# The rotary half exchange of the prompt's queries on ScalarE instead of TensorE, and a later wait for parked rows, in a one-layer hybrid decoder step

## The reference, cut to what matters

```python
def rope(x, pos):
    half = ROPE_DIM // 2                      # 32
    ...
    x1, x2 = x[..., :half], x[..., half:]
    return jnp.concatenate([x1 * cos - x2 * sin, x1 * sin + x2 * cos], axis=-1)

q = jnp.einsum('bsc,chd->bshd', rmsnorm(qa, g_q_a), w_q_b)       # 16 heads of 128 + 64
q_nope, q_pe = q[..., :NOPE_DIM], rope(q[..., NOPE_DIM:], q_pos)
...
# PEER: the 2048 numbers of a token are projected to 8 heads x 2 x 128 query numbers,
# each scored against 128 sub keys; the 16 best of each half are combined
q = jnp.einsum('td,dhpk->thpk', hb, w_peer_query)
s = jnp.einsum('thpk,hpnk->thpn', q, peer_sub_keys)
s1, i1 = lax.top_k(s[:, :, 0], PEER_TOPK)
s2, i2 = lax.top_k(s[:, :, 1], PEER_TOPK)
```

## Time and profile before

| | us |
|---|---|
| median of 3 runs (lowest, highest) | 4596.78 (4593.75, 4599.67) |
| the profiled execution's own time | 4598.26 |
| its span on the core | 4596.5 |

### The profile page before, as it was taken

How to read it: one execution, slowest core, us unless ns; L and a number is a source line. 1 busy time by engine, 2 the same in 40 slices (tenths; PEclk the granted TensorE clock), 3 DMA queues, 4 the chain that set the end, 5 groups by cost and what they waited for, 6 DMA issues and landing times.

```text
span 4596.5 us, 37965 instructions
## 1 busy us (share of the span) xinstructions
PE 3684.4 (80%) x13918; PEld 2303.6 (50%) x13918; DVE 2780.5 (60%) x3641; ACT 392.1 (9%) x882; POOL 1493.0 (32%) x1217
## 2 busy tenths in 40 slices
PE   8999999987999999999999999999999980000000
PEld 6888846652999585555555456444444430000000
DVE  3224323431000168887676578888965569999998
ACT  1012123321000010000000010000000000000000
POOL 0000100024000013444454445434332227777763
PEclk9999999998999999999999999999999995555555
DMA  4121261137667678998999989999999999999998
GB/s 167 65 74 65 102 235 42 42 126 251 230 239 245 230 289 309 395 400 366 403 421 411 367 366 388 403 406 403 395 412 393 423 423 409 401 410 410 410 412 364
DMA packets 223666, 1413.36 MB, mean 307 GB/s; under 512 B 33312, under 2 KB 42400, under 8 KB 59488
## 3 DMA queue, kind: packets, MB, share of 16 engines
q0 software_dynamic: 137424, 904.11, 48.5%
q1 hardware_dynamic: 72768, 471.37, 26.9%
q10 hardware_dynamic: 13296, 35.52, 2.0%
HBM read 1385.11 MB, written 25.75 MB: 307 GB/s over the span
## 4 chain that ended last, share of the span: by engine, by line
PE 71%; DMA 13%; POOL 5%; issue 5%; DVE 4%; ACT 1%; SPq 0%; ACTq 0%; DVEq 0%; POOLq 0%
PE psum L975 25%; PE psum L1116 13%; PE psum L627 12%; DMA arena<-in_v,arena 12%; PE psum L1095 4%; POOL arena L582 3%; DVE psum L2062 3%; POOL arena L602 2%; PE psum L1080 2%; PE psum L1043 1%; PE psum L1023 1%; PE psum L699 1%; PE psum L709 1%; PE psum L869 1%; PE psum L868 1%
## 5 line engine op out<-in xcount | busy, mean ns | idle before, releaser
L975 PE MATMUL psum<-arena 128*128 128x160 f32 (+1 forms) x5120 | 1175.7, 393 | 1.0 <-DVE arena L1746 0.8
L975 PEld LDWEIGHTS psum<-arena 128*128 128x128 f32 x5120 | 835.7, 190 | 340.5 <-DVE arena L1746 0.9
L2062 DVE SCALAR_TENSOR_TENSOR psum<-arena,psum 128x2048 f32<-128x2048 f32 x381 | 897.1, 2355 | 165.2 <-DMA arena<-in_v,arena 155.7
L582 POOL DMA_INDIRECT arena<-in_v,arena x544 | 648.4, 1192 | 744.0 <-DVE psum L2062 327.1
L1116 PE MATMUL psum<-arena 128*128 128x512 f32 x2048 | 881.8, 593 | 0.6 <-ACT arena L1433 0.6
L582 POOL DMA_INDIRECT arena<-in_u,arena x288 | 479.2, 1664 | 1228.3 <-DVE arena L1853 516.2
L1116 PEld LDWEIGHTS psum<-arena 128*128 128x128 f32 x2048 | 390.0, 190 | 491.9 <-issue 491.9
L627 PE MATMUL psum<-arena 128*128 128x272 f32 x2432 | 562.0, 392 | 0.9 <-issue 0.9
L627 PEld LDWEIGHTS psum<-arena 128*128 128x128 f32 x2432 | 460.8, 190 | 98.8 <-issue 5.5
L1940 DVE SCALAR_TENSOR_TENSOR arena<-arena,pages 128x2048 f32<-128x2048 f32 x128 | 301.1, 2352 | 72.1 <-DMA arena<-in_v,arena 67.3
L1897 DVE CUSTOM_DVE_ANT_1 arena<-arena 128x2048 f32<-128x2048 f32 x128 | 288.5, 2289 | 55.8 <-DMA arena<-in_u,arena 54.8
(11 more groups left out here) (298 smaller groups left out, 2678.6 us busy)
## 6 DMA issues: line engine op xcount, KB each, us to landing
arena<-in_w_merge SPq DMA_DIRECT2D x160, 1024.0 KB, 5.6
arena<-in_u_cols SPq DMA_DIRECT2D x128, 1024.0 KB, 9.3
arena<-in_w_out SPq DMA_DIRECT2D x32, 1024.0 KB, 4.9
arena<-in_w_query SPq DMA_DIRECT2D x32, 1024.0 KB, 6.9
arena<-in_w_proj SPq DMA_DIRECT2D x31, 1024.0 KB, 4.9
products<-arena ACTq DMA_DIRECT2D x32, 512.0 KB, 13.6
arena<-in_pool_keys SPq DMA_DIRECT2D x64, 192.0 KB, 3.6
arena<-in_v,arena POOLq DMA_INDIRECT x544, 12.0
```

The costliest lines, as they stand in the source:

```text
L582: pool.indirect_dma_start(row, None, A[table], bass.IndirectOffsetOnAxis(ap=idx[:, r:r + 1], axis=0))\
L975: last = mm(out, w[:, (off + k) * P:(off + k + 1) * P], src[:, k0 + k, lo:hi], start=(k == 0), stop=(k == n - 1))
L2062: V.scalar_tensor_tensor(a, four(row), atmp_b[:, t, r:r + 1], a if r else four(x1_b[:, t, :]), ALU.mult, ALU.add).then_inc(s("rows_used"), 1)
```

## The change

1. The two permutation matmuls of a pair are gone. `values(0, 2)` now carries the ring signal that the first of them carried, and `values(2, 4)` follows at once.
2. ScalarE copies `pair(3)` four times, 32 partitions by 544 columns each, into `ropt` with the halves exchanged, ahead of its copy to `qraw`. VectorE waits for `q_stored` instead of `q_swapped`, and its first operation reads and writes `ropt` in SBUF instead of reading PSUM.
3. In part a's query loop ScalarE waits for the parked rows in step 1, ahead of the first kept scores, instead of ahead of the loop.

```diff
-                values(0, 2)
-                pe.wait_ge(s("q_stored"), n * 3 + 3)
-                mm(pair(3)[:, 0, :], swap, qraw[:, 0:HALF], start=True, stop=True).then_inc(ring_used, 1)
-                mm(pair(3)[:, 1, :], swap, qraw[:, HALF:T], start=True, stop=True).then_inc(s("q_swapped"), 1)
+                values(0, 2).then_inc(ring_used, 1)
                 values(2, 4).then_inc(s("kv_ready"), 1)
...
                     act.wait_ge(s("q_ready"), n * 3 + 3)
+                    for b in range(4):
+                        a_(halves(ropt)[32 * b:32 * b + 32], pair(3)[32 * (b ^ 1):32 * (b ^ 1) + 32], ACT.Copy)
                     a_(halves(qraw), pair(3), ACT.Copy).then_inc(s("q_stored"), 1)
...
-            act.wait_ge(s("parked"), 48)
             for u in range(17):
...
                 if u >= 1:
                     act.wait_ge(s("scored"), u)
+                    if u == 1:
+                        act.wait_ge(s("parked"), 48)
                     a_(scores_s[0:SAMP, u - 1, :], psum[0:SAMP, (3, 4)[(u - 1) % 2], 0:P], ACT.Copy).then_inc(s("scores_kept"), 1)
...
-                    dve.wait_ge(s("q_swapped"), n + 1)
-                    V.tensor_tensor(halves(ropt), pair(3), halves(sin), ALU.mult).then_inc(s("q_turned"), 1)
+                    dve.wait_ge(s("q_stored"), n * 3 + 3)
+                    V.tensor_tensor(ropt, ropt, sin, ALU.mult).then_inc(s("q_turned"), 1)
```

## The result

| | before | after |
|---|---|---|
| median of 4 runs, us (lowest, highest) | 4596.32 (4593.75, 4599.67) | 4669.06 (4662.98, 4673.95) |
| the profiled execution's own time, us | 4598.26 | 4669.64 |
| its span, us | 4596.5 | 4667.9 |

The ratio after to before is 1.0151 (95% interval 1.0140 to 1.0163): the change made the kernel 73 us slower, where 4 us less were forecast, and the time lies far outside the range of 4588.5 to 4600.0.

A forecast was written before the change was run, and what follows sets the result against it. TensorE was taken to bound the attention loop from end to end, with rotary slack of about 0.1 us per pair. 4598.3 - 4.9 (parked wait) + 0.5 (loop) = 4593.9 us, as a median 4592.4 us; range 4588.5 to 4600.

The forecast's parts named there:

- What bounds the loop: Attention loop: TensorE is the chain from end to end, 37.91 us per pair, rotary chain slack about 0.1 us.
- the chain that takes over: Each loop pair: ScalarE's copies, then VectorE's three operations, release TensorE at 745.47 against 745.44.
- The matmuls' time comes back: Rival, attention loop: 0.91 us per pair, 7.3 us in all, regained in full; 4584.6 us, chance 0.04.
- The copies' cadence: Attention loop, ScalarE: neighbouring copies of 544 columns start 0.52 us apart, also those of 32 partitions.
- the copies don't overlap: Rival, attention loop: changing start partitions keep ScalarE's copies from overlapping, loop loses 3.8 us; 4595.7 us, chance 0.14.
- the pricing of the new wait: TensorE ahead of the scores: waits the 0.91 us saved; pair 0.03 to 0.1 us longer, 0.5 us lost over the loop.
- the rival alone: Attention loop: clock falls behind TensorE's new wait of 0.9 us in each pair; 4607.5 us, chance 0.06.
- The price: Clock fall per loop pair: 1.89 us, taken from the stall at 1618 in part a's queries.
- The chance: 0.06 for the clock falling in the loop; 0.72 us idle at 1026 to 1027 had left it at 1.00.
- The parked wait: Start of part a's queries: the 3.0 us stall and 1.89 us of slow clock behind it go, 4.9 us gained.

The follow-up runs named there:

- the run without the exchange: Kernel before without the two permutation matmuls per pair and with no copies in their place, VectorE using unexchanged numbers; 4649.85 us against 4668.06.
- The run with dense work behind the wait: Changed kernel with eight idle matmuls of 512 columns between TensorE's wait for the rotary chain and the scores; 4656.07 us, kernel before 4598.19.
- the copies alone: Changed kernel with the wait for the parked rows back in its old place; ratio to the kernel before 1.0149, 4725.66 against 4655.78 us.
- the later VectorE: Kernel before, permutation matmuls kept, with two idle products of 544 columns ahead of VectorE's first rotary product; 4704.53 us against 4668.06.
- the kernel with the new order: Changed kernel with the `qraw` copy ahead of the four exchanged copies and VectorE's cosine product ahead of the sine one; ratio 1.0003, 4657.51 against 4655.78 us.
- the parked-only kernel: Kernel before with only the later wait for the parked rows; ratio 0.9995, 4652.18 against 4655.78 us.

## Why the prediction was wrong

**What bounds the loop, and the chain that takes over.** Right. The time of the two matmuls went into a new wait of TensorE for VectorE, as told. The matmuls' time comes back only where nothing waits: 0.96 us per pair in the run without the exchange, where 0.91 was read.

**The copies' cadence** was mis-sized: 0.52 us forecast, 0.62 measured. This moved the wait from 0.9 to 1.32 us and cost 0.4 us per pair, 3.3 us in all. The rival "the copies don't overlap" (0.14) named this, and its reason; its time of 4595.7 us was still far off. The Trainium skill, "VectorE: DVE Perf Modes", section on two Vector instructions with no wait between them, states for VectorE only that a change of the start partition holds an instruction back; on ScalarE the copies with changing starts (0.62 us apart) and those with one start (0.50) came out as that rule has it. The Trainium skill, "ScalarE: Activation LUTs", section on what a table load costs, gives an overlap of about 93 ns: with one start partition the traces have some more (0.62 long, 0.50 apart: about 0.12 us), with changing ones none.

**The step that failed** is the pricing of the new wait: "The 0.91 us saved are spent in a new wait, and the pair becomes 0.03 to 0.1 us longer." The pair became 9.9 us longer: 0.4 by the longer wait, and so some 9.5 through the clock. The mechanism stood among the rivals with a chance of 0.06 and a price of 1.89 us per pair. The price was five times too low, and with the right one the rival alone would have given a time of about 4668 us (4592.4 + 8 x 9.5), against 4669.06 measured.

The price came from a stall behind which dense matmuls follow. There the clock was back after some 4 us:

```profile
1624.00:1625.00 1.00, 1.00 (x5) 1.00 (x5) 0.78 (x4) 0.00 (x0) 0.00 (x0) 0.50 0.03 8
1625.00:1626.00 1.00, 1.00 (x9) 1.00 (x8) 0.05 (x1) 0.00 (x0) 0.00 (x0) 0.89 0.00 0
```

Behind this wait follow the score matmuls, and there the clock stayed at 0.50 for 20 us. The run with dense work behind the wait shows the difference: back within 4 us, with the same wait, and 1.7 us lost where the clock fell. So 1.89 us is about the right price for a fall ahead of dense work and the wrong one here.

The chance came from waits that left the clock at 1.00, and from the belief that only longer ones bring it down. The runs refute that: waits of 0.65 us (3 pairs of 8), 0.89 us (4 of 8), 1.41 us (5 of 8) and, with dense work behind, 1.32 us (4 of 8) each brought it down in some pairs and not in others of the same kernel. A few short waits without a fall say little, where there will be one in each of eight pairs.

**The parked wait.** Right in mechanism and size inside the stage: 5.5 us gained where 4.9 were forecast. Measured alone over the whole kernel it gave 3.6 us, which the interval doesn't tell from none.

**What stays open.** Why the changed kernel falls in all eight pairs, where others with like waits fall in about half. By the clock records of the traces, the 32 falls behind this wait in all kernels came 0.3 to 2.5 us after it ended. In the changed kernel the fall keeps its place, 1.1 us behind the wait in the first pair and 0.8 in the last, and with the copies alone 0.5 to 0.3 us from the second pair on, while in the kernels where only some pairs fall the distance moves about (0.8 to 2.1 us with the later VectorE). So every pair of the changed kernel may meet whatever decides it in the same state as the last, but that is argued, not tested. What it is about the score matmuls that keeps a fallen clock down isn't shown either: the same stage holds a clock of 1.00 in every pair that didn't fall. Why the kernel with the new order gains nothing in total is open as well.

## What to carry to other kernels

Matmuls taken off TensorE save nothing where another engine's chain ends 0.1 us before TensorE needs it, and the wait that takes their place can cost many times its length (9.5 us for a wait of 1.32), if the clock falls and the work behind doesn't bring it back. So fill such a place with work that doesn't depend on the late operand, here the position-free scores, or shorten the late chain by starting what is ready first. Both together, on top of the later parked wait, gave 8.9 us of gain on the chip where the exchange by copies alone lost 70; of the two, filling the place is the safer, since a short wait of 0.65 us still cost three pairs their clock. Read the price of a fallen clock from a stretch with the same kind of work behind it.

## What the runs showed of the hardware

- The granted clock fell behind TensorE waits as short as 0.65 us, and in the same kernel left other pairs with the same wait alone.
- At 0.50 the profile shows TensorE busy for 2.00 of 2.00 us over the score stage, and the clock still stayed down for 20 us; with dense matmuls in that place it was back within 4 us, and the score stage behind them then kept 1.00.
- ScalarE copies of 544 columns are 0.50 to 0.52 us apart when all start at partition 0, and 0.62 when neighbours start at other partitions. A copy of 32 partitions took 0.61 us and one of 128 took 0.62.
- The kernel before took 4598, 4656 and 4668 us on three chips (the first and last a single run). Only the one of the result was profiled. The attention loop of the parked-only kernel was as long as its own, but the merge's first matmul, behind the gathers of cached pages, began at 1210.0 us in the parked-only kernel against 1174.8 in the kernel before.
